# Two copies moved on ScalarE inside the stick-breaking attention of a two-block kernel

## What is computed

```python
h = xn @ w_in
b_c, c_c, h_c, q, k, v, g_conv, g_attn = jnp.split(h, ...)
y_conv = b_c * causal_dwconv(c_c * h_c, conv_w_mix)
# per head, 16 heads of 64
z = q @ k.T / 8                                  # scores
log_beta = jax.nn.log_sigmoid(z)
log_fail = jnp.where(causal, log_beta - z, 0.0)  # = -softplus(z), masked
survive = lax.cumsum(log_fail, reverse=True) - log_fail
a = jnp.where(causal, jnp.exp(log_beta + survive), 0.0)
o = a @ v
```

## Time and profile before

| | |
|---|---|
| median of 3 runs | 1920.56 us |
| the profiled execution's own time | 1920.75 us |
| its span (first to last instruction) | 1919.0 us |
| TensorE busy | 1790.4 us, 93% of the span |
| VectorE / ScalarE / GpSimd busy | 56% / 47% / 11% |
| chain that ended last | PE 63%, DVE 15%, ACT 8%, issue 7%, DMA 4% |
| eight passes of mixing | from about 57 us to 498 us of the span |

### The profile page before, as it was taken

The page is one execution under the profiler, slowest core; times in us unless marked ns, Lnnn a source line. Parts: engine busy times, 40 slices in busy tenths (PEclk is TensorE's granted clock), DMA queues, the critical chain, the costliest instruction groups (busy, mean ns, idle before and its releaser), DMA issues.

```text
span 1919.0 us, 31049 instructions
## 1 busy us (share of the span) xinstructions
PE 1790.4 (93%) x11869; PEld 1579.1 (82%) x11869; DVE 1071.2 (56%) x1612; ACT 902.8 (47%) x1190; POOL 204.4 (11%) x362
## 2 busy tenths in 40 slices
PE   5899999999999996999999987799899999899996
PEld 4899999999999995999998855688677777788884
DVE  4455555556333358555544348886567677645443
ACT  4566766676533344333332232255455655633332
POOL 0011111011000010800005740100000000000001
PEclk8999999999999998999999999899999999999998
DMA  3222222222122252322224414944111211233322
GB/s 116 87 77 67 66 87 66 77 87 78 62 92 89 96 163 70 100 87 91 95 95 133 143 68 170 217 140 123 56 50 61 78 65 55 77 99 103 133 95 97
DMA packets 71441, 182.81 MB, mean 95 GB/s; under 512 B 22916, under 2 KB 23108, under 8 KB 71240
## 3 DMA queue, kind: packets, MB, share of 16 engines
q1 hardware_dynamic: 68824, 172.89, 28.8%
q0 software_dynamic: 2544, 8.91, 1.3%
HBM read 162.62 MB, written 16.80 MB: 93 GB/s over the span
## 4 chain that ended last, share of the span: by engine, by line
PE 63%; DVE 15%; ACT 8%; issue 7%; DMA 4%; SPq 2%; POOL 1%; ACTq 0%; DVEq 0%
PE J L796 24%; PE J L1035 14%; PE J L808 6%; PE J L1006 6%; DMA WR<-weights 3%; DVE WL L1742 2%; PE J L1205 2%; PE J L1156 1%; POOL E L2421 1%; ACT E L1355 1%; ACT E L1351 1%; PE J L1072 1%; PE Z L882 1%; SPq L709 1%; DVE MX L2296 1%
## 5 line engine op out<-in xcount | busy, mean ns | idle before, releaser
L1742 DVE TENSOR_TENSOR WL<-WR,WH 128x1024 fp32r<-128x1024 f32 x271 | 343.8, 1269 | 292.1 <-ACT WH L1284 282.4
L1284 ACT ACTIVATE WH<-WR 128x1024 fp32r<-128x1024 f32 x271 | 285.5, 1054 | 229.3 <-DMA WR<-weights 101.3
L796 PE MATMUL J<-XH,WH 128*128 128x264 f32 (+1 forms) x1376 | 286.1, 289 | 26.6 <-DVE XL L1746 18.8
L796 PE MATMUL J<-XH,WL 128*128 128x264 f32 (+1 forms) x1376 | 280.9, 286 | 0.0
L796 PE MATMUL J<-XL,WH 128*128 128x264 f32 (+1 forms) x1376 | 280.9, 286 | 0.0
L796 PEld LDWEIGHTS J<-XH,WH 128*128 128x128 f32 x1376 | 217.2, 191 | 33.0 <-issue 20.3
L796 PEld LDWEIGHTS J<-XL,WH 128*128 128x128 f32 x1376 | 215.9, 191 | 0.0
L796 PEld LDWEIGHTS J<-XH,WL 128*128 128x128 f32 x1376 | 215.2, 191 | 0.0
L2421 POOL TENSOR_SCALAR_AFFINE_SELECT E<-E 128x128 f32<-128x128 f32 (+1 forms) x160 | 52.5, 365 | 446.3 <-DVE E L1814 238.8
L1035 PE MATMUL J<-X2H,WH 128*128 128x512 f32 x168 | 71.2, 424 | 15.7 <-DVE X2L L2116 9.2
L2439 POOL TENSOR_TENSOR SA<-SQ 128x512 f32<-128x512 f32 (+1 forms) x3 | 3.9, 1298 | 703.8 <-ACT SQ L1528 513.5
(11 more groups left out here) (451 smaller groups left out, 4224.8 us busy)
## 6 DMA issues: line engine op xcount, KB each, us to landing
WR<-weights SPq DMA_DIRECT2D x271, 512.0 KB, 3.5
cp_dram<-CQR POOLq DMA_DIRECT2D x8, 288.0 KB, 2.5
cp_dram<-CQI POOLq DMA_DIRECT2D x8, 288.0 KB, 2.4
CPR<-cp_dram SPq DMA_DIRECT2D x8, 288.0 KB, 4.0
CPI<-cp_dram SPq DMA_DIRECT2D x8, 288.0 KB, 4.2
X<-tokens SPq DMA_DIRECT2D x4, 528.0 KB, 5.2
H<-tokens SPq DMA_DIRECT2D x8, 264.0 KB, 4.0
res_dram<-H SPq DMA_DIRECT2D x1, 2048.0 KB, 8.0
```

The costliest lines, as they stand in the source:

```text
L796: mm = pe.matmul(o[:, 512 * h:512 * h + half], ws[:, s, w], xs[:, a:a + half], start=(k == 0 and i == 0), stop=(k == 7 and i == 2))
L1284: act.activation(WH[:, n % SPLIT, :], WR[:, n % RAW, :], ACT.Copy).then_inc(w_hi, 1)
L1742: dve.tensor_tensor(WL[:, n % SPLIT, :], WR[:, n % RAW, :], WH[:, n % SPLIT, :].bitcast(F32), ALU.subtract).then_inc(w_lo, 1)
```

## The change

Three moves, nothing added or removed:

1. On ScalarE, `softplus` takes a function `between` and calls it after the exponential and ahead of the logarithm. Both heads pass their `head_out`, that is the wait for the value sums (`pv_done`) and the copy `OH`. It stood behind the logarithm before.
2. On ScalarE, in the even head, the copy of the C job's result to `CT` stands ahead of `fail_hi(h)` (the split of the log weights, `LH` and `GH`). It stood behind it before.
3. On VectorE, `head_out` (the subtraction `OL`) stands ahead of `softplus`. It stood behind it before. In pass 0, where there is no head to take out, the `nop` that frees the tile moves with it.

```diff
--- before.py
+++ after.py
@@ -1342,7 +1342,7 @@
             split_hi(SPLIT)
             k_hi_(T_MIX + 2, N_MIX + 1)
 
-            def softplus(h):
+            def softplus(h, between=None):
 
                 h = as_lin(h)
                 act.wait_ge(z_done, val(h + 1))
@@ -1351,6 +1351,8 @@
                 act.activation(E[:], Z[:, 0:SCORE], ACT.Abs).then_inc(soft_step, 1)
                 act.wait_ge(soft_step, val(3 * h + 1))
                 act.activation(E[:], E[:], ACT.Exp, scale=-1.0).then_inc(soft_step, 1)
+                if between is not None:
+                    between()
                 act.wait_ge(soft_step, val(3 * h + 2))
                 act.activation(E[:], E[:], ACT.Ln, bias=1.0).then_inc(soft_step, 1)
 
@@ -1396,14 +1398,12 @@
                     act.wait_ge(vt_done, val(m))
                 act.activation(halves(VT[:]), src, ACT.Copy).then_inc(read_out[(t + 4) % 2], 1)
                 split_hi(n + 4)
-                softplus(h)
-                if later:
-                    head_out(h - 1, m - 1, t + 5)
-                fail_hi(h)
+                softplus(h, (lambda: head_out(h - 1, m - 1, t + 5)) if later else None)
                 src = job_result(t + 6, n + 1)
                 if positive(m):
                     act.wait_ge(y_lo, val(m))
                 act.activation(halves(CT[:]), src, ACT.Copy).then_inc(read_out[(t + 6) % 2], 1)
+                fail_hi(h)
                 split_hi(n + 5)
                 act.wait_ge(vt_done, val(m + 1))
                 if positive(h):
@@ -1419,8 +1419,7 @@
 
                 act.wait_ge(read_out[slot(t + 9)], nth(t + 9) + 1)
                 act.activation(YH[:, cols(m * L1, L1)], CT[:], ACT.Copy).then_inc(y_hi, 1)
-                softplus(h + 1)
-                head_out(h, m, t + 10)
+                softplus(h + 1, lambda: head_out(h, m, t + 10))
                 fail_hi(h + 1)
                 if not last:
                     q_hi(m + 1, t + 11, n + 6)
@@ -1858,11 +1857,11 @@
                 if later:
                     weight_lo(h - 1)
                 split_lo(n + 4)
-                softplus(h)
                 if later:
                     head_out(h - 1, m - 1, t + 5)
                 else:
                     dve.nop().then_inc(read_out[(t + 5) % 2], 1)
+                softplus(h)
                 fail_lo(h)
                 split_lo(n + 5)
                 dve.wait_ge(v_hi, val(m + 1))
@@ -1890,10 +1889,10 @@
                 dve.tensor_tensor(halves(CT[:]), JV[(t + 9) % 2], halves(CV[:]), ALU.mult)\
                    .then_inc(read_out[(t + 9) % 2], 1)
                 split_lo(n + 9)
-                softplus(h + 1)
                 dve.wait_ge(y_hi, val(m + 1))
                 low(YL[:, cols(m * L1, L1)], CT[:], YH[:, cols(m * L1, L1)]).then_inc(y_lo, 1)
                 head_out(h, m, t + 10)
+                softplus(h + 1)
                 fail_lo(h + 1)
                 if not last:
                     q_lo(m + 1, t + 11)
```

## The result

The changed kernel took **1943.59 us** (median of four runs, 1942.16 to 1944.97) against 1920.03 (four runs, 1919.16 to 1924.77): a ratio of 1.0111 with a 95% interval of 1.0096 to 1.0126 (the two medians alone give 1.0123). I had forecast 1924.4 within 1916 to 1928 and given 0.22 to "slower by over 0.3%". The kernel is slower, clearly so: by 23.6 us where I forecast about 4. The profiled execution took 1942.66 us, with a span of 1940.9.

What follows compares the result with a forecast made beforehand. TensorE, busy 93% of the span, was taken as the bound, so only its few microseconds of waits could be won. 1920.75 - 3.5 - 1.55 + 1.2 + 7.1 + 0.6 = 1924.6, as a median 1924.4 us, range 1916 to 1928.

Steps and rivals of the forecast that it cites:

- (a): Mixing passes 1 to 6: all six TensorE waits for OL within reach go, 3.5 us won.
- (d): Passes 1 to 6, even head's values: TensorE waits for AL, late by 1.25 us, 7.1 us lost.
- (e): Pass 7, even head's values: a wait for the late AL beyond 0.88 us of slack, 0.6 us lost.
- (f): Odd head: LL comes up to 1.9 us later, but the running sums have 2.5 us of room, costed at nothing.
- (b): Pass 0: waits for nop and C copy go, values of head 0 start 1.66 us earlier, 1.55 us won.
- (c): Pass 0: the new wait of 2.4 us ahead of the values brings a slow clock, 1.2 us lost.
- R2: Rival: each new wait in passes 1 to 7 drops the clock to 0.50, 1.2 us seven times, 1932.8; chance 0.09.

Runs made afterwards that it cites:

- p0_only: The kernel before with only the two moves of pass 0 (C copy ahead of the split, nop ahead of softplus): 1924.59 us, ratio 1.0009.
- delay_13: The kernel before, order untouched, with an added ScalarE copy of a whole tile (1440 columns) ahead of the even head's split AH: 1944.49 us, ratio 1.0121.
- delay_07: The kernel before, order untouched, with an added ScalarE copy of half a tile (720 columns) ahead of the even head's split AH: 1932.84 us, ratio 1.0054.
- ct_late: The full change with the C copy back behind the split of the log weights and done twice: 1931.57 us, ratio 1.0046.
- head_only: The full change without the C copy's move, which stays behind the split of the log weights: 1926.64 us, ratio 1.0022 against the kernel before.
- odd_only: The kernel before with the head's copy moved between exponential and logarithm, and OL ahead of softplus, in the odd head alone: 1919.08 us, ratio 0.9980.
- scores_wait: The kernel before with TensorE's wait for AL placed ahead of the odd head's scores: 1962.05 us, ratio 1.0188.
- fill: The full change plus ten unread 128 x 256 matmuls on TensorE between the odd head's scores and the even head's values: 1928.14 us, ratio 1.0022.
- ct_only: The kernel before with the C copy alone moved ahead of the split of the log weights: 1944.0 us, ratio 1.0124.

## Why the prediction was wrong

Right, step by step: the waits that go (a); the delay of the even head's chain, 1.25 said and 1.20 (`LH`) and 1.30 (`AL`) measured, through both copies, the weight landing and the table load; the new waits, 5.8 us in passes 1 to 6 where (d) said 6.5, and 0.34 in pass 7 where (e) said 0.5; nothing from the odd head (f). Of (b), the values of pass 0 started 0.9 us earlier (89.13 against 90.04) where I said 1.66; with the moves of pass 0 alone (p0_only) they start at 88.38, as worked out, and why they are later in the full change stays open.

The step that failed is the price of an idle TensorE, in (c) and in (d) and (e). Two things were wrong with it.

First its size. I took the cost of a fall from one case, 1.2 us behind the wait of 2.67 us in pass 0, where the low clock lasted 2.8 us of matmuls. In the full change it holds through most of windows of 7.2 to 9.0 us and cost 3.0 to 4.6 us a time. In pass 0 the values alone took 6.07 us instead of 3.34, and the jobs behind them 1.3 more.

Second its condition. I read a threshold out of two rows, "the clock stayed behind 1.4 us and fell behind 2.67", and put it between them as if idle time were what counts. So I gave R2, the rival in which each new wait brings the clock down, a chance of 0.09 and wrote that the new waits lie below the threshold. R2 is what happened, in four of the seven passes 1 to 7, and with pass 0 in five of eight; but at its 1.2 us a time R2 itself gave only 1932.8. The two rows came from places where a long row of 258- or 264-column matmuls followed the wait. The new waits lie in the middle of the short ones. At that place 0.85 to 1.10 us was enough in four passes of six (full change), 1.29 and less in five of seven (delay_13), and 0.67 or less not once (the one trace of delay_07). Ahead of the H job 1.24 to 1.42 us never was (seven waits in the one trace of ct_late).

One of the two rows was luck besides. The wait of 1.44 us for the last head's `OL`, from which I took "the clock stayed", is the same instruction with the same wait in every one of the fourteen traces. The short value sums of the last head stand ahead of it, matmuls of 258 columns behind it. Before (first line) and in seven others the clock stays at 1.00 behind it; in six (head_only, odd_only, delay_07, delay_13, scores_wait, fill) it is 0.50 in a stretch of about 3 us there, as in odd_only (second line):

```profile
508.90:512.30 3.40, 3.37 (x28) 1.00 0.19 77
504.00:507.40 3.40, 3.07 (x14) 0.50 0.28 114
```

So no threshold of idle time could be read from one row, and one execution does not tell whether a given wait brings the clock down.

The sum with the right price: 1920.75 - 3.5 (waits for `OL`) + 6.2 + 0.7 (waits for `AL`, restarts) + 17.7 (falls) - 0.9 (values of pass 0 start earlier) = 1941, against 1942.66. The remaining 1.7 us lie within what the untouched stages vary (they took 1.8 us more here than before). The 17.7 is no independent number: it was read from the lengths of the passes themselves.

What the Trainium skill states on its page "TensorE: Matmul & The Clock Gate", section "Part 1: The HAM clock gate", had pointed the right way: it states that the clock gate is set by how busy TensorE has been recently. The traces agree as far as this: of the windows behind the new waits five are at 0.51 to 0.59, and with ten matmuls in the wait's place the clock stayed at 1.00. I used it for one term of pass 0, and did not ask how busy TensorE is around each of the seven other waits.

What stays open: which waits of one length at one place are followed by a fall. 1.05 and 1.10 us (passes 1 and 5) had none where 0.85 (pass 6) had one, and scores_wait had none in pass 6 at 1.46 where 1.45 in pass 5 had one; pass 3 had one in the full change at 0.87 and none in ct_only at 0.93. No run tells these apart. Also not separated is whether it is what stands ahead of the wait or behind it, the few columns, the 64 rows or the share of weight loads that makes the stretch of scores and values sensitive.

## What to carry to other kernels

Before moving anything ahead of an instruction on a lightly loaded engine, follow that instruction's result to where TensorE picks it up: here 26 us, four engines and a weight landing later, with 0.36 us of slack. If TensorE then idles, do not price the wait by its length alone: look at what stands on both sides of it, take the clock from several traces and not from one row, and compare TensorE's busy time for the same matmuls: if it grows, the clock is the cost and not the wait. Of a change in several parts try each alone: here one part wins 4 us and another loses 24.

## What the runs showed of the hardware that was not expected

- A wait of about 1 us between short matmuls was in four passes of six followed by 1.2 GHz for so long that it cost 3.0 to 4.6 us (full change), while seven waits of 1.24 to 1.42 us ahead of the 264-column H job left the clock at 1.00 (ct_late).
- One and the same wait of 1.44 us, at the end of mixing, had the clock at 0.50 behind it in six of fourteen traces and at 1.00 in eight.
- Ten matmuls without a use in place of the idle time kept the granted clock at 1.00, and were worth some 15 us (1928.14 against 1943.59).
- An idle time of TensorE ahead of the H job costs 0.2 to 0.3 us more than its label (passes of 56.90 us in ct_late: 55.2, a wait of 1.4 and 0.3), one ahead of the values less than 0.1 (passes of 56.3 and 56.1 us in the full change with no fall: 55.2, waits of 1.01 and 0.85, and 0.06).
